# Two ring places per weight transfer in the expert stages: 16 KB runs instead of 8 KB

## The reference, cut to what matters

```python
def expert_choice_ffn(h, router, w_gate, w_up, w_down):
    bsz, t, d = h.shape
    cap = CAPACITY_FACTOR * t // N_EXPERTS
    aff = jax.nn.softmax((h @ router).astype(jnp.float32), axis=-1)
    gates, idx = lax.top_k(jnp.swapaxes(aff, 1, 2), cap)
    xs = jax.vmap(lambda hb, ib: hb[ib])(h, idx)
    a = jnp.einsum('becd,edf->becf', xs, w_gate)
    u = jnp.einsum('becd,edf->becf', xs, w_up)
    y = jnp.einsum('becf,efd->becd', jax.nn.silu(a) * u, w_down)
    y = y * gates[..., None].astype(y.dtype)
    return jax.vmap(lambda ib, yb: jnp.zeros((t, d), yb.dtype).at[ib.reshape(-1)].add(yb.reshape(-1, d)))(idx, y)
```

## Time and profile before

| what | value |
|---|---|
| median of 3 runs | 2575.14 us |
| profiled execution, its own time | 2572.74 us |
| its span in the trace | 2570.9 us |
| TensorE (PE) busy | 2194.1 us, 85% |
| VectorE / ScalarE / GpSimd busy | 767.1 / 609.1 / 741.6 us |
| granted TensorE clock, mean | 0.914 |
| moved by DMA | 635.92 MB, mean 247 GB/s |

### The profile page before, as it was taken

The page is one execution under the profiler, slowest core; times in us unless marked ns, Lnnn a source line. Parts: engine busy times, 40 slices in busy tenths (PEclk is TensorE's granted clock), DMA queues, the critical chain, the costliest instruction groups (busy, mean ns, idle before and its releaser), DMA issues.

```text
span 2570.9 us, 31126 instructions
## 1 busy us (share of the span) xinstructions
PE 2194.1 (85%) x12134; PEld 1410.9 (55%) x12134; DVE 767.1 (30%) x1442; ACT 609.1 (24%) x889; POOL 741.6 (29%) x624
## 2 busy tenths in 40 slices
PE   7988889989798899989798999999989876565655
PEld 6866778878686779765455444444447542121211
DVE  4844220123522211356643122222246530000001
ACT  3534323433633234211332000000011410000000
POOL 7736346778372577810300000000010100000000
PEclk9989889999899899999898999999989887878776
DMA  8324658754146487341102899999972149999996
GB/s 265 132 83 163 213 172 293 244 177 148 66 164 231 162 292 273 125 178 66 66 1 98 331 421 422 422 422 422 421 267 100 65 182 421 421 422 422 422 422 278
DMA packets 171521, 635.92 MB, mean 247 GB/s; under 512 B 10040, under 2 KB 16440, under 8 KB 122120
## 3 DMA queue, kind: packets, MB, share of 16 engines
q1 hardware_dynamic: 168368, 623.79, 62.9%
q0 software_dynamic: 2608, 9.25, 1.4%
q10 hardware_dynamic: 424, 1.22, 0.1%
HBM read 633.17 MB, written 1.05 MB: 247 GB/s over the span
## 4 chain that ended last, share of the span: by engine, by line
PE 65%; DMA 16%; DVE 10%; ACT 3%; POOL 3%; issue 3%; SPq 1%; DVEq 0%; ACTq 0%
PE bank L1207 16%; PE bank L544 8%; PE bank L546 8%; PE bank L545 8%; DMA ring<-in_w_up 7%; PE bank L1038 4%; DMA ring<-in_w_down 3%; PE bank L1161 3%; DMA ring<-in_w_gate 3%; PE bank L1221 3%; POOL ring_r L1371 3%; PE bank L1231 3%; PE bank L720 2%; DMA ring<-in_ffn_w_gu 2%; PE bank L1047 2%
## 5 line engine op out<-in xcount | busy, mean ns | idle before, releaser
L1371 POOL TENSOR_TENSOR ring_r<-ring,ring_r 128x512 fp32r<-128x512 f32 (+1 forms) x544 | 674.7, 1279 | 384.1 <-ACT ring_r L1467 323.4
L1207 PE MATMUL bank<-ring,arena 128*64 128x512 f32 (+1 forms) x3024 | 586.4, 710 | 180.0 <-DMA ring<-in_w_up 60.6
L544 PE MATMUL bank<-ring_r 128*128 128x256 f32 (+1 forms) x1504 | 469.6, 312 | 41.4 <-DVEq L1945 27.5
L1207 PEld LDWEIGHTS bank<-ring,arena 128*64 128x64 f32 (+1 forms) x3024 | 175.0, 141 | 571.2 <-issue 555.7
L546 PE MATMUL bank<-xT_r,ring_r 128*128 128x256 f32 x1248 | 358.6, 287 | 0.0
L545 PE MATMUL bank<-ring_r 128*128 128x256 f32 x1248 | 357.3, 286 | 0.0
L1467 ACT ACTIVATE ring_r<-ring 128x2048 fp32r<-128x2048 f32 (+1 forms) x138 | 253.0, 1839 | 401.2 <-PE bank L546 205.1
L544 PEld LDWEIGHTS bank<-ring_r 128*128 128x128 f32 x1504 | 293.7, 195 | 67.6 <-DVEq L1945 30.1
L546 PEld LDWEIGHTS bank<-xT_r,ring_r 128*128 128x128 f32 x1248 | 244.4, 196 | 0.0
L545 PEld LDWEIGHTS bank<-ring_r 128*128 128x128 f32 x1248 | 243.3, 195 | 0.9 <-issue 0.7
L1400 POOL TENSOR_TENSOR arena<-const 128x1024 f32<-128x1024 f32 x6 | 12.1, 2021 | 667.2 <-DVEq L1945 595.2
(11 more groups left out here) (322 smaller groups left out, 2621.2 us busy)
## 6 DMA issues: line engine op xcount, KB each, us to landing
ring<-in_w_down SPq DMA_DIRECT2D x128, 1024.0 KB, 18.5
ring<-in_w_up SPq DMA_DIRECT2D x126, 1024.0 KB, 18.1
ring<-in_w_gate SPq DMA_DIRECT2D x124, 1024.0 KB, 16.5
ring<-in_ada_w SPq DMA_DIRECT2D x48, 1024.0 KB, 6.5
ring<-in_ffn_w_gu SPq DMA_DIRECT2D x40, 1024.0 KB, 5.3
ring<-in_ffn_w_down SPq DMA_DIRECT2D x20, 1024.0 KB, 5.1
ring<-in_mem_wkv SPq DMA_DIRECT2D x16, 1024.0 KB, 5.1
ring<-in_w_in SPq DMA_DIRECT2D x16, 1024.0 KB, 14.2
```

The costliest lines, as they stand in the source:

```text
L544: pe.matmul(dst, w_hi, v_hi, start=first, stop=False)
L1207: mm = pe.matmul(dst[nb][W * j:W * j + W, :], src[:, 2 * q + c, W * j:W * j + W], rooms[j][:, c, UN * nb:UN * nb + UN], start=(q == c == 0 ...
L1371: pool.tensor_tensor(lo[:, c], whole[:, c], hi_of(u)[:, c, 0:n], ALU.subtract).then_inc(*signal("w_lo", (u, c)))
```

## The change

From the second group of experts on, one transfer fills two ring places with four rows per partition (rows 4h to 4h+3, one run of 16 KB), for one expert and one half h of a matrix; so the order within a matrix is half, then expert (`pair_order`). Only the down product of the last group is still loaded by quarters into single places. The wait of `product` is once per half, for the pair; a quarter takes its two rows out of it. SP waits for the second quarter of a half before it loads over a pair (`pair_read`). The semaphore of the even place of a pair counts for both, so the counts are taken from a list, `ring_signals`. The first group is loaded as before. Matmuls, their order and all other engines' instructions stay.

```diff
+def pair_order(layer):
+    g = experts_per_group(layer)
+    return [(name, h, j) for name in ("w_gate_2", "w_up_2", "w_down_2") for h in range(2) for j in range(g)]
+
+def pair_read(layer, p):
+    g = experts_per_group(layer)
+    return 4 * (p // (2 * g)) + 2 * (p % (2 * g) // g) + 2
...
+                in_pairs = key[0] == "experts" and len(moe_units(key[1])) <= k < count - len(moe_units(key[1])) // 3
+                if not (in_pairs and slot % 2):
+                    signalled[slot] += 1
+                ring_signals.append(signalled[slot])
...
+        def pair_of(slot):
+            return ring[:, slot:slot + 2].rearrange("p u a b -> p (u a b)").rearrange("p (c n) -> p c n", c=4)
...
+        def pair_home(layer, p):
+            v = group_at(layer) + 2 * p
+            return pair_of(v % RING), ring_in[v % RING], 16 * ring_signals[v]
...
-                            room, loaded, n = expert_home(layer, k) if first else ring_home(layer, k)
-                            pe.wait_ge(loaded, n if first else i * (16 * U // RING) + n)
+                            if first or (last and bi == 2):
+                                room, loaded, n = (expert_home if first else last_home)(layer, (4 * bi + q) * G + j)
+                                pe.wait_ge(loaded, n)
+                            else:
+                                pair, loaded, n = pair_home(layer, (2 * bi + q // 2) * G + j)
+                                if q % 2 == 0:
+                                    pe.wait_ge(loaded, (i - 1) * (16 * U // RING) + n)
+                                room = pair[:, 2 * (q % 2):2 * (q % 2) + 2]
...
-                    steady = len(homes) + RING
-                    for k in range(len(homes), steady):
+                    for k in range(len(homes), U):
...
-                    with sp.Fori(0, loops) as i:
-                        for k in range(steady, steady + U):
-                            read_through(i * 12 + ((k - RING) // G + 1))
-                            load(k, *ring_home(layer, k)[0:2], i)
...
+                    def load_pair(i, p):
+                        name, h, j = pair_order(layer)[p]
+                        room, loaded, _ = pair_home(layer, p)
+                        view = w[name][layer, i * G + (j + G)].rearrange("(p c) n -> p c n", c=KC)
+                        sp.dma_start(room, view[:, 4 * h:4 * h + 4, :]).then_inc(loaded, 16)
+
+                    with sp.Fori(0, groups - 2) as i:
+                        for p in range(U // 2):
+                            ahead = p - RING // 2
+                            read_through(i * 12 + (pair_read(layer, ahead) + 12 if ahead >= 0 else pair_read(layer, ahead + U // 2)))
+                            load_pair(i, p)
+                    for p in range(U // 3):
+                        ahead = p - RING // 2
+                        read_through((groups - 2) * 12 + (pair_read(layer, ahead) + 12 if ahead >= 0 else pair_read(layer, ahead + U // 2)))
+                        load_pair(groups - 2, p)
+                    for k in range(2 * U // 3, U):
+                        ahead = k - RING
+                        read_through((groups - 1) * 12 + (pair_read(layer, ahead // 2) if ahead < 2 * U // 3 else ahead // G + 1))
+                        load(k, *last_home(layer, k)[0:2], groups - 1)
```

More of the change, by code:

```diff
@@ L193, in build @@
     unit_at, n = {}, 0
-    ring_pos, unit_of_pos = {}, []
+    ring_pos, unit_of_pos, ring_signals, signalled = {}, [], [], [0] * RING
     for key, _ in units:
@@ L200, in build @@
                 ring_pos[n + k] = len(unit_of_pos)
+                slot = len(unit_of_pos) % RING
                 unit_of_pos.append(n + k)
+                in_pairs = key[0] == "experts" and len(moe_units(key[1])) <= k < count - len(moe_units(key[1])) // 3
+                if not (in_pairs and slot % 2):
+                    signalled[slot] += 1
+                ring_signals.append(signalled[slot])
         n += count
@@ L380, in slot_of @@
             v = ring_pos[u]
-            return v % RING, ring_in[v % RING], 16 * (v // RING + 1)
+            return v % RING, ring_in[v % RING], 16 * ring_signals[v]
         def wide_of(slot):
             return ring[:, slot].rearrange("p a b -> p (a b)").rearrange("p (c n) -> p c n", c=2)
+        def pair_of(slot):
+            return ring[:, slot:slot + 2].rearrange("p u a b -> p (u a b)").rearrange("p (c n) -> p c n", c=4)
         def expert_home(layer, k):
@@ L399, in expert_home, with group_at, last_home @@
             v += homes[:k].count("ring") if k < len(homes) else k - len(homes) + homes.count("ring")
[L400 to L406, removed]
+            return wide_of(v % RING), ring_in[v % RING], 16 * ring_signals[v]
+        def group_at(layer):
+            homes = first_homes(layer)
+            return ring_pos[unit_at[("experts", layer)]] + homes.count("ring") - len(homes) + len(moe_units(layer))
+        def pair_home(layer, p):
+            v = group_at(layer) + 2 * p
+            return pair_of(v % RING), ring_in[v % RING], 16 * ring_signals[v]
+        def last_home(layer, k):
+            v = group_at(layer) + len(moe_units(layer)) * (NE // experts_per_group(layer) - 2) + k
+            return wide_of(v % RING), ring_in[v % RING], 16 * ring_signals[v]
         def hi_of(u):
@@ L1193, in _, with product @@
                         pe.wait_ge(bank_free[b8], filled[b8])
-                def product(i, bi, dst, src, first):
+                def product(i, bi, dst, src, first, last):
                     for q in range(4):
@@ L1199, in product @@
                         for j in range(G):
-                            k = (4 * bi + q) * G + j
-                            room, loaded, n = expert_home(layer, k) if first else ring_home(layer, k)
-                            pe.wait_ge(loaded, n if first else i * (16 * U // RING) + n)
+                            if first or (last and bi == 2):
[6 more added lines that the diff above has]
+                                room = pair[:, 2 * (q % 2):2 * (q % 2) + 2]
                             rooms.append(room)
@@ L1236, in group @@
                     pe.wait_ge(m["xt"], i + 1)
-                    product(i, 0, (bank[0], bank[1]), moe_x, not before)
+                    product(i, 0, (bank[0], bank[1]), moe_x, not before, not more)
                     if before:
@@ L1242, in group @@
                     mm.then_inc(m["g_full"], 1)
-                    product(i, 1, (bank[2], bank[3]), moe_x, not before)
+                    product(i, 1, (bank[2], bank[3]), moe_x, not before, not more)
                     if more:
@@ L1252, in group @@
                     pe.wait_ge(m["ht_sb"], 2 * i + 2)
-                    product(i, 2, (bank[4], bank[5]), moe_hT, not before)
+                    product(i, 2, (bank[4], bank[5]), moe_hT, not before, not more)
                 gather(0)
@@ L1305, in _ @@
                         load(k, *expert_home(layer, k)[0:2], 0)
-                    steady = len(homes) + RING
-                    for k in range(len(homes), steady):
+                    for k in range(len(homes), U):
                         read_through((unit_of_pos[ring_pos[u + k] - RING] - u) // G + 1)
                         load(k, *expert_home(layer, k)[0:2], 0)
-                    loops, rest = divmod(U * groups - steady, U)
-                    with sp.Fori(0, loops) as i:
-                        for k in range(steady, steady + U):
-                            read_through(i * 12 + ((k - RING) // G + 1))
-                            load(k, *ring_home(layer, k)[0:2], i)
@@ L1315, in _ @@
-                    for k in range(steady, steady + rest):
-                        read_through(loops * 12 + (k - RING) // G + 1)
-                        load(k, *ring_home(layer, k)[0:2], loops)
+                    def load_pair(i, p):
[3 more added lines that the diff above has]
+                        sp.dma_start(room, view[:, 4 * h:4 * h + 4, :]).then_inc(loaded, 16)
@@ L1318, in _ @@
+                    for k in range(2 * U // 3, U):
+                        ahead = k - RING
+                        read_through((groups - 1) * 12 + (pair_read(layer, ahead // 2) if ahead < 2 * U // 3 else ahead // G + 1))
+                        load(k, *last_home(layer, k)[0:2], groups - 1)
                     for k in range(U):
-                        moe_last[u + U * (groups - 1) + k] = (m["quarters"], (groups - 1) * 12 + k // G + 1)
+                        moe_last[u + U * (groups - 1) + k] = (m["quarters"], (groups - 1) * 12 + (pair_read(layer, k // 2) if k < 2 * U // 3 else k // G + 1))
```

## The result

The changed kernel takes 2613.44 us (median of 4 runs, 2607.95 to 2615.06) against 2575.59 (4 runs, 2575.08 to 2576.99): ratio 1.0144, 95% interval 1.0129 to 1.0158, so 37 us slower by the ratio and 37.9 by the medians. The prediction was 2603, range 2573 to 2621.

The account below looks back on a forecast made before the run. Layer 1 was taken as bound by transfers alone, layer 0 on the edge, on TensorE's side; 2572.7 + 27 (layer 1) + 1 (layer 0) = 2600.7, with 2.4 us for timed runs 2603, range 2573 to 2621.

Parts of the forecast that it names:

- Packets: DMA loads: 16 KB runs save 9.3 ns per packet saved, 1.5% at best, at most 4.8 us in layer 1.
- fixed cost of 2.0 us per transfer: DMA loads of layer 1: paid one after the other, 64 saved transfers would be worth 128 us; set aside as hidden.
- The dry queue in layer 1: Layer 1: places return late, the DMA stands about 2 us per half, 21.7 us against 19.88; +27 us in sum.
- The burst: TensorE in layer 1: two quarters read after some 12 us of idle, starting at low clock, taken as 9.4 us.
- The rest of the turn: Layer 1, per half: 0.2 us to issue, 1.6 restart, 9.8 for two pairs, 0.7 from last data to TensorE's start.
- The two ends of layer 1: Layer 1: first paired half starts 1.7 us earlier; the turn to the last down product costs 1.8 us more.
- Layer 0: Layer 0: gate loads keep 1.3 us of lead; waits of 0 to 2 us, taken as +1, bound +8.
- Rival A: Layer 1: TensorE reads both quarters at full clock, the queue never stands; 2568.6 us, faster; chance 0.14.
- knife-edge of 9.1 against 9.1 us: Layer 1: full-clock reading, issue and restart, 7.28 + 0.2 + 1.6 us, equal the 9.1 us of transfers in flight.
- 0.7 us for the landing: Layer 1: TensorE starts 0.7 us behind the slowest DMA engine's last data, as a dry queue lets it catch up.
- B: Both layers: 16 KB runs are no faster; 2.4 us more in layer 1, layer 0 +6, about 2610 us; chance 0.16.
- C: Layer 1: dry queue costs more, burst 10.2 us, landing 1.5 us, half 23.3 us; +53, 2629 us; chance 0.10.
- the forecast's case: Whole kernel: 2603 us, within 2585 to 2612, with layer 1 bursts of 8.3 to 9.9 us; chance 0.53.

Follow-up runs that it names:

- e4: The changed kernel plus matmuls without use ahead of each wait for a half in layer 1: 2599.92 us, ratio 1.0107 against before.
- e5: Layer 0 as before; layer 1 in pairs, but TensorE reads two experts at a time and each chunk frees 4 places: 2569.86 us for 2573.77 before.
- e6: e5 with each pair loaded by two 1 MiB transfers of 8 KB runs: 2572.74 us for 2573.77 before.
- e3: The changed kernel's order, waits and late freeing in both layers, but each pair in two 1 MiB transfers of 8 KB runs: 2612.13 us, ratio 1.0143 against before.
- e7: e5, but SP frees the places of both chunks only when the half's second chunk is read: 2596.44 us for 2574.37 before.
- e1: The change in layer 1 alone, layer 0 loading single places as before: 2604.98 us for 2572.98 before.
- e2: The change in layer 0 alone, layer 1 loading single places as before: 2576.20 us for 2572.98 before.

## Why the prediction was right, point by point

- **Packets.** Predicted 4.89 us per 2 MiB, 429 GB/s, from the cost per packet of 2 and 8 KB runs. Measured 425 to 429 in layer 0 (419 to 426 in the one trace of e4), 428 to 429 in layer 1 of e5. Right as a rate. That the cost is one per packet, rather than per transfer, was argued from the step from 2 to 8 KB and isn't tested by itself. The worth in layer 1 was put at 4.8 us at most; e5 against e6 gives 2.9. The fixed cost of 2.0 us per transfer, which the prediction weighed and set aside, plays no part here: by the prediction's own reckoning it would have made 128 us, where e5 against e6 shows 2.9. The page that it comes from (the Trainium skill, "DMA: Bandwidth & Descriptors", section on the anatomy of one DMA) gives it for transfers issued from GpSimd, which the prediction didn't say; SP issues these.
- **The dry queue in layer 1.** The mechanism is as forecast: e3 has it without long runs, e5 loses it by returning places in fours (0.1 us of idle engine time in 295 us, for 27.8 in 328), e7 has two thirds of the loss back by returning them late (20 us for the 30 of e1). The turn was put at 21.7 us and measured 21.9 (328.52 us over 15, from 2214.62 to 2543.14). Two terms were off and nearly cancel, so part of the closeness is luck. The burst was taken as 9.4 us and had a mean of 8.99 in these turns. The rest of the turn, 0.2 + 1.6 + 9.8 + 0.7 = 12.3, measured 12.35 to 12.58 in 11 of 15 turns, and 13.1, 13.7, 14.7 and 14.9 in the other four, on the mean 12.9. One of the long ones, from 2323.99, returns in e1 at the same place (2324.28 to 2347.82). It isn't a slower restart: SP had issued at 2332.99, 0.3 us behind the burst, and the engines stood idle for 1.4 us, less than the mean. But in this turn and in the other of over 14 us (from 2498.32) one packet was always under way, and behind the next burst the engines began to run dry 6.7 and 6.3 us after its start, where it is 8.8 to 8.9 in ten of the 15. So the last engine was some 3 us behind the first ones, and the landing came late by it. Why it lags just there stays open.
- **The two ends of layer 1.** The first half was to be 1.7 us earlier than the second quarter of before. It was 0.3 (2214.62 less the 4.76 us that this execution was already late): the landing came later than counted. The turn to the last down product was to cost 1.8 us and cost 0.3 (21.71 for 21.41): the two quarters of before were already 21.41 us apart there, which the trace of before shows and the working left out. The sum, -0.3 + 30.3 + 0.3, is 30.3 for 27.
- **Layer 0.** Predicted 0 to 2 us of waiting, taken +1; the trace has two waits of 0.5 us and bursts of 27.9 to 28.0 us for 27.69, 2.6 in all, and e2 says 4 (0.8 to 7) by its ratio and 2.1 in its trace. Right in kind, mis-sized by 1 to 3: a lead of 1.3 us was left for the gate pair of group 2 by the reckoning, and the pair came 0.5 us late. That a slower rate costs about 6 us there was borne out by e3's waits of 5.9. The term isn't a constant of the kernel, as e4's waits of 4.5 us with the same code show.
- **Rival A** (a warm burst saves the queue) falls. The bursts were not warm: the granted clock is 0.50 from 2270 us on and still when the burst of 2279.55 begins. And where a reading took 7.06 or 7.07 us (four turns of e4, eight of e7) the next half came 20.7 to 22.4 us later, not 19.6. The knife-edge of 9.1 against 9.1 us on which it rested counts the work in flight from the last of the 16 engines, with 0.7 us for the landing, "as a dry queue lets the slow engine catch up". That term was the mis-sized one for a queue that doesn't run dry: in e4's turn from 2296.30 it doesn't, and at the next landing the first engines were 2.4 us ahead of the last. A reading at the full clock does help, though: in e7 the engines stand idle for 0.7 us in such turns and 2.6 in the others.
- **Rivals B and C.** B is out: where the queue is full, 16 KB runs flow at 425 to 429 in all traces but e4's. Of C, a late landing is what four of the 15 turns had, and 1.5 us for it fits the mean better than 0.7 did; but its burst of 10.2 us was never reached (longest 9.98). The measured time lies between the forecast's case and C.
- **What the sum did not hold.** It forecast +28 us; the median rose by 37.9, the profiled execution by 35.2. Layer 1 has 3.3 of the difference and layer 0 1.6. Another 3.7 lie ahead of the first down product of layer 0, in matmuls that are the same, less 1.5 between the stages. And the changed kernel's median lies 5.5 us above its profiled execution, where the prediction added 2.4. The start of the layer 0 stage's gather (1403.80 before, 1406.01 after) is at 1408.75 in e1, 1408.65 in e2, 1410.78 in e3 and 1402.20 in e4, so one profile can't place a few us.

## What to carry to other kernels

When a ring feeds an engine that is faster than the DMA, count what is in flight at the moment a block has landed: ring size less the places that the block holds until it is read. It must last longer than the reading at the clock that the engine really has after its idle, plus the restart, and it must be counted for the DMA engine that ends first, not for the last one, which releases the reader: 9.8 us in flight were not enough for a reading of 7, as the first engines ran dry 6.1 to 9.0 us after the landing in e7. Longer transfers and the size of the block that is waited for are two choices; e5 took the first (1.5% of rate, 3 us here) and made the block smaller by reading fewer experts over more rows, which an idle TensorE can afford.

## What was not expected of the hardware

- The 16 DMA engines drift apart by microseconds, and a landing waits for the last. In the changed kernel the engines began to run dry 6.3 to 8.9 us after a landing that had left 9.8 us in flight. The two turns in which the queue never went wholly empty handed on the largest lags, 3.1 and 3.5 us.
- A restart has two prices. In the turn from 2257.44 the first packet starts 1.0 us after the issue, and the first packets then take 1.0 to 1.5 us instead of 0.61; over the 15 turns this second part is 10.0 us beside 27.8 of idle engine time.
- With half of the array's columns used for twice as long, TensorE's granted clock is 0.94 to 0.98 in layer 1 (stretches of e5 from 2240 to 2500), where bursts between waits have 0.78 to 0.79 (before) and 0.70 to 0.75 (after). Reading all four experts at once saves no time when the DMA sets the pace.
